# Expert weights of a routed layer loaded as three 2 MB transfers per tile in place of six of 1 MB

## The reference

```
def expert_block(args):
    xblk, e = args
    return (jax.nn.silu(xblk @ w_gate[e]) * (xblk @ w_up[e])) @ w_down[e]
# w_gate, w_up: (32, 1024, 512)   w_down: (32, 512, 1024)   float32, 2 MB each
y = jnp.sum(yb[dest].reshape(T, TOP_K, D) * gate[..., None], axis=1)
```

## Time and profile before

| | before |
|---|---|
| median of 3 runs | 1345.14 us (1344.77 to 1346.2) |
| profiled execution | 1343.46 us |
| its span, first to last instruction | 1341.7 us |
| PE, DVE, ACT, POOL busy in the span | 1172.6, 920.0, 597.2, 219.8 us |
| granted TensorE clock, mean | 0.932 |
| expert weight loads | 210 of 1 MB (six of them before the loop) |
| HBM read, written | 271.44 MB, 26.74 MB |

### The profile page before, as it was taken

One profiled execution on the slowest core, in us unless ns is written; L12 is line 12 of the kernel. 1 busy time (PEld: TensorE's weight loads), 2 busy tenths in 40 slices (PEclk: granted clock), 3 DMA queues, 4 the chain that ended last, 5 costly groups with the idle time before them and its releaser, 6 DMA issues.

```text
span 1341.7 us, 14343 instructions
## 1 busy us (share of the span) xinstructions
PE 1172.6 (87%) x5061; PEld 883.9 (66%) x5061; DVE 920.0 (69%) x788; ACT 597.2 (45%) x593; POOL 219.8 (16%) x253
## 2 busy tenths in 40 slices
PE   3999999999975899943699999999999999999920
PEld 2344445888852788832588888888888888888820
DVE  4125796455566111158399999999999999999846
ACT  2130100222223111130378777777777777777622
POOL 3200000101110000002032222221222222222121
PEclk9899999999987899965799999999999999999975
DMA  7310111000011011131399999999999999999637
GB/s 256 100 32 31 32 65 60 0 1 1 1 50 75 32 63 64 47 141 62 124 388 378 377 386 377 409 395 383 396 369 367 370 375 361 385 369 365 244 126 254
DMA packets 63439, 278.78 MB, mean 208 GB/s; under 512 B 11543, under 2 KB 25949, under 8 KB 36524
## 3 DMA queue, kind: packets, MB, share of 16 engines
q1 hardware_dynamic: 49408, 251.67, 50.0%
q0 software_dynamic: 10544, 18.08, 3.7%
q10 hardware_dynamic: 3452, 8.55, 1.6%
HBM read 271.44 MB, written 26.74 MB: 222 GB/s over the span
## 4 chain that ended last, share of the span: by engine, by line
PE 47%; DMA 3%; DVE 1%; ACT 0%; issue 0%; SPq 0%; POOLq 0%; POOL 0%
PE ps L1340 15%; PE ps L1342 15%; PE ps L1341 15%; PE ps L1335 2%; DMA yk<-expert_rows 2%; PE ps L1357 1%; DMA xg<-hf_rows,now_g 1%; DVE x L1111 0%; DVE x L1114 0%; DMA expert_rows<-ym,now_s 0%; DVE xm_lo L1045 0%; DVE w_lo L1040 0%; SPq L393 0%; ACT xm_hi L698 0%; ACT w_hi L692 0%
## 5 line engine op out<-in xcount | busy, mean ns | idle before, releaser
L1040 DVE TENSOR_TENSOR w_lo<-raw,w_hi 128x2048 fp32r<-128x2048 f32 x210 | 474.2, 2289 | 48.0 <-ACT w_hi L692 46.6
L692 ACT ACTIVATE w_hi<-raw 128x2048 fp32r<-128x2048 f32 x210 | 399.1, 1919 | 21.8 <-PE ps L1342 21.7
L1340 PE MATMUL ps<-w_hi,xm_hi 128*128 128x512 f32 x560 | 224.2, 400 | 3.7 <-DVE xm_lo L1045 3.7
L1341 PE MATMUL ps<-w_lo,xm_hi 128*128 128x512 f32 x560 | 220.6, 394 | 0.0
L1342 PE MATMUL ps<-w_hi,xm_lo 128*128 128x512 f32 x560 | 220.6, 394 | 0.0
L1171 PE MATMUL ps<-xnT,raw 128*128 128x512 f32 x384 | 168.0, 599 | 1.2 <-PE ps L1171 1.2
L808 DVE SCALAR_TENSOR_TENSOR acc<-uT,pcol,acc 128x1024 f32<-128x1024 f32 x120 | 154.0, 1284 | 3.6
L1171 PEld LDWEIGHTS ps<-xnT,raw 128*128 128x128 f32 x384 | 73.1, 192 | 96.1 <-issue 95.1
L1340 PEld LDWEIGHTS ps<-w_hi,xm_hi 128*128 128x128 f32 x560 | 105.9, 189 | 27.1 <-DVE xm_lo L1045 4.4
L1342 PEld LDWEIGHTS ps<-w_hi,xm_lo 128*128 128x128 f32 x560 | 105.6, 189 | 24.8
L1341 PEld LDWEIGHTS ps<-w_lo,xm_hi 128*128 128x128 f32 x560 | 105.7, 189 | 22.7
(11 more groups left out here) (214 smaller groups left out, 1196.5 us busy)
## 6 DMA issues: line engine op xcount, KB each, us to landing
raw<-in_expert_w_up_dram SPq DMA_DIRECT2D x70, 1024.0 KB, 7.5
raw<-in_expert_w_down_dram SPq DMA_DIRECT2D x70, 1024.0 KB, 7.3
raw<-in_expert_w_gate_dram SPq DMA_DIRECT2D x70, 1024.0 KB, 7.5
raw<-in_w_in_dram SPq DMA_DIRECT2D x10, 1024.0 KB, 6.0
yk<-expert_rows SPq DMA_DIRECT2D x16, 512.0 KB, 4.9
xa<-in_x_dram SPq DMA_DIRECT2D x8, 512.0 KB, 7.0
xin<-in_x_dram SPq DMA_DIRECT2D x8, 512.0 KB, 3.2
raw<-in_w_out_dram SPq DMA_DIRECT2D x4, 1024.0 KB, 5.0
```

The lines of the kernel that those rows point to most:

```text
L692: act.activation(w_hi[:, slot, :], raw[:, i, :], ACT.Copy).then_inc(hi_rdy, 1)
L1040: dve.tensor_tensor(w_lo[:, slot, :], raw[:, i, :], w_hi[:, slot, :].bitcast(F32), ALU.subtract)\
L1340: pe.matmul(dst, x_hi, w_hi[:, s, cols], start=first, stop=False)
L1341: pe.matmul(dst, x_hi, w_lo[:, s, cols], start=False, stop=False)
```

## The change

SP loads gate, up and down as one transfer each into the two neighbouring buffers of the kind (0 and 1, 2 and 3, 4 and 5). The wait before it is for the `w_lo` of the second buffer. The landing is told by the semaphore of the first buffer alone, and ACT waits on that one for both halves. The first expert (line 348) is still loaded in six pieces. Bytes, layout in the buffers, the splits and all matmuls are as before.

```diff
+        def expert_pairs(e):
+
+            return [(0, wg_v[e]), (2, wu_v[e]), (4, wd_v[e])]
+
-            def load_piece(i, v, n_lo):
+            def load_pair(i, v, n_lo):
+
                 sp.wait_ge(lo_rdy, n_lo)
-                sp.dma_start(raw[:, i, :].rearrange("p (j n) -> p j n", n=D if i >= 4 else F), v)\
+                sp.dma_start(raw[:, i:i + 2, :].rearrange("p r (j n) -> p (r j) n", n=D if i >= 4 else F), v)\
                     .then_inc(raw_in[i], 16)
 
             def load_gate_up(e, w):
-                for i in range(4):
-                    load_piece(i, expert_pieces(w)[i], i + 1 if isinstance(e, int) and e == 1 else 6 * e - 7 + i)
+                for i, v in expert_pairs(w)[0:2]:
+                    load_pair(i, v, i + 2 if isinstance(e, int) and e == 1 else 6 * e - 6 + i)
 
             def load_down(e, w):
-                for i in (4, 5):
-                    load_piece(i, expert_pieces(w)[i], piece_no(e, i) - 5)
+                for i, v in expert_pairs(w)[2:3]:
+                    load_pair(i, v, piece_no(e, i) - 4)
 
...
-                        for i in range(6):
-                            load_piece(i, expert_pieces(e)[i], 6 * (j + NE) - 5 + i)
+                        for i, v in expert_pairs(e):
+                            load_pair(i, v, 6 * (j + NE) - 4 + i)
...
             def split_hi(e, i, slot, n):
-                act.wait_ge(raw_in[i], 16 * (front_uses[i] + 1) + 16 * e)
+                r = i if first(e) else i // 2 * 2
+                act.wait_ge(raw_in[r], 16 * (front_uses[r] + 1) + 16 * e)
```

## The result

| | before | changed |
|---|---|---|
| median | 1344.95 us (1343.47 to 1346.2, 4 runs) | 1357.83 us (1356.18 to 1360.35, 4 runs) |
| profiled execution, its span | 1343.46, 1341.7 us | 1360.35, 1358.6 us |

The ratio is 1.0099, 95% interval 1.0085 to 1.0113: some 13 us slower. I had forecast no change, 1345.6, with 1343.4 to 1354.0 as the range. The time lies beyond the range, on the side of rival (a).

What follows compares the result with a forecast made beforehand. PE's matmul stream was taken to set the pace, not the loads. Steady stage 0, start +0.3 and drain +0.2 made +0.5 us, a median of 1345.6 us, counted as no change; the range was 1343.4 to 1354 us.

Steps and rivals of the forecast that it cites:

- rival (a): Slower: gate's loop, landing plus 8.84 us, exceeds the 17.97 us tile; at a 9.4 us landing +5.6, 1351; chance 0.26.
- part 1: Per tile, three issues of 0.33 us and three SyncE waits fewer; worth nothing, as SyncE idles between them.
- Part 2: The steady stage: pairs go out later and land whole, but in time for their users; cost 0.
- the budgets (8.92 us for gate): Steady stage, time from a pair's issue to ACT's first copy: 9.96 us up, 10.28 down, 8.92 gate, the tight one.
- critical landing of 9.13: Steady stage: gate's own loop exceeds the tile once its landing takes over 17.97-8.84 = 9.13 us.
- landing of 8.1 us: Steady stage, gate pair from issue to landing: 7.5 us in a nearly empty queue plus 0.56 for a scatter; ends 7.5 and 10.0.
- capacity: Steady stage: pairs, gather and scatter need 15.9 to 17.3 of 17.97 us; about a tenth of the DMA rate is free.
- slack of 3.3 us: Steady stage: w_lo is ready 3.3 us before PE starts a tile's second and fourth pieces, so one late landing costs nothing.
- Part 3: Start of the stage: first gather, queued 5.3 us among tile 1's loads, changes by +0.3 us, ends -1 and +2.5.
- Part 4: The drain: last down pair issued at 1269.63 lands at 1277.1, wanted at 1276.94; +0.2 us, ends 0 and +0.5.
- Rival (b): Faster: larger pieces move faster and the first gather comes through early; half of 5.3 us gives 1342.5; chance 0.05.
- Rival (c): The 2 MB are cut up on the way and only the issue is later; same time, inside the forecast, no own chance.

Runs made afterwards that it cites:

- late start alone: The kernel before, still with six 1 MB transfers, but both halves of a kind issued only when the second buffer is free; ratio 1.0017.
- half-down run: The changed kernel with only the first half of every down matrix loaded, 1 MB, gate and up still whole pairs; ratio 1.0009.

## Why the prediction was wrong

- **What bounds the kernel before, and part 1:** right. PE had no wait, and half as many issues gave nothing back.
- **Part 2, the budgets (8.92 us for gate) and the critical landing of 9.13:** borne out. With gate at 8.1 us, or at 7.8, the tiles stay at 18.0; with 9.3 they don't. The 8.84 us of rival (a) that follow a landing were measured 16 times, at 8.81 to 8.88.
- **Part 2, the landing of 8.1 us: the step that failed.** I wrote that the down pair ahead is through "by about 953.9", 7.5 us after its issue, "so the queue is nearly empty". 7.5 is what I had for a lone pair, and also the median of a 1 MB piece in traffic; neither is a pair of 2 MB behind up's pair. Down landed in 11.0 us, 3.5 later than I had it, and gate in 9.3. I counted gate's own later start and let the pairs ahead of it behave as if nothing stood before them. In the kernel with the gate pair alone 8.1 is right to the tenth, but that is in part luck: there the down pieces take 9.6 us, so the queue isn't nearly empty at that time either. The half-down run shows the rest: with a shorter queue ahead the same pair lands in 7.8. (A piece of 1.049 MB at 426 GB/s is 2.46 us and not 2.47; nothing hangs on it.)
- **Part 2, capacity ("about a tenth of the rate is free"):** it says nothing about a landing. The late start alone still moved 378 GB/s, and the 371 of the changed kernel follow from its longer tiles. What failed was the time of single transfers, not the sum of their bytes.
- **The slack of 3.3 us:** right as a reserve for one late landing, wrong as an argument for zero, because the landings were late in nearly every tile (25 waits for gate in some 30). I had said so in rival (a). The sign of being wrong that I had named, PE waiting for `w_lo` and tiles over 18.0 us, is what came. `x_lo`, with 3.0 us, was missing from my list of slack; PE waited for it too, 2.3 us in five waits.
- **Rival (a)** was the right mechanism at a chance of 0.26, and its price was too low: by its sum a landing of 9.3 to 9.4 costs 2 to 6 us, and the stage lost 11.4. It took one landing for all tiles, where they swing from 8.2 to 11.0, and the seven longest steps carry most of the loss. About 3 of the 13 us came through scatters, which I had set down only at tile 3. How the rest divides between the swing and the slack stays open. The upper end of 10.0 that I turned down is the median over gate and down together.
- **Part 3:** the first gather ended at 645.73 against 645.28, forecast +0.3; but it was issued 1.4 us earlier in this execution (633.19 against 634.62), so the change cost it 1.9 us, within my ends of -1 and +2.5. The 5.3 us of queueing were real; 4.4 of them could be had.
- **Part 4, the drain:** +0.2 forecast, +2.9 measured from the last transposes. The last down pair landed 7.7 us after its issue, as I had it (7.5), at 1289.6. ACT, held by the scatter above until 1289.90 and then by two short copies, came to it at 1290.88, 1.2 us later. With two result buffers the drain was at +1.3. So that wait, not in my list, is about half of the miss; the other half is unexplained.
- **Rival (b)**, faster by larger pieces, found nothing; nor did the Trainium skill's rule of at least 1 MiB per transfer ("DMA: Bandwidth & Descriptors", Rules for kernel authors), which both kernels meet: 1 MB pieces reached 426 GB/s.
- **Rival (c):** the 2 MB transfer did what it says, in runs of 16 KB.

## What to carry to other kernels

A larger transfer into the same buffers spends the lead twice: it starts when the last buffer is free, and it can be used when the last byte is in. Each may fit the slack alone and not together, so sum them for all streams at once and let each transfer's own later landing be the queue of the next. Write the loop as landing plus what follows it, and set it against the pace with the slowest landings as well as with the median. Where loads and a transfer on the chain share the engines, look for loads that can simply wait: that was worth 0.36% here, where the larger transfers only lost.

## What the runs showed of the hardware

- The landing of one and the same transfer goes by what stands ahead of it: the 2 MB of gate landed in 9.4 us behind 2 MB of down, in 8.1 among 1 MB pieces and in 7.8 behind 1 MB of down (medians of 700:1240), and in 8.2 to 11.0 within one execution.
- Runs of 8 KB in place of 16 KB didn't shorten the landing of 2 MB (gate 9.7 and 9.4 us in that window, one profile each).
- POOL's scatter instruction takes 0.97 to 7.15 us. Both ends of it that were looked at in the changed kernel came 0.9 us after the end of DVE's uninterrupted subtractions of two SBUF operands (1282.77 after 1281.90, and 1209.93 after 1209.04). The Trainium skill says why ("GPSIMD Engine Reference", section Specifications): GpSimd shares its SBUF interfaces with VectorE and contends with instructions that have two SBUF inputs. The rows agree.
